# Prompt attention in a hybrid decoder step: items turned and weighed in batches of two, and narrow units scored into four single banks

## What is computed

```python
def attend_shared(q, k, v, dist, valid, rel_bias):
    logits = jnp.einsum('bqhgd,bkhd->bqhkg', qg, k).astype(jnp.float32) * ATTN_SCALE + bias
    p = masked_softmax(logits, valid[None, :, None, :, None])
    o = jnp.einsum('bqhkg,bkhd->bqhgd', p.astype(v.dtype), v)
...
def nsa_combine(gates, o_c, o_s, o_w):
    return gates[..., 0:1] * o_c + gates[..., 1:2] * o_s + gates[..., 2:3] * o_w
```

## Time and profile before

| | us |
|---|---|
| median of 3 runs (985.49 to 988.01) | 987.76 |
| span of the profiled execution, first to last instruction | 983.7 |
| median less that span (start and end of the program) | 4.06 |
| prompt attention within the span (its units and items) | 555.7 to 826.9 |

### The profile page before, as it was taken

One profiled execution on the slowest core, in us unless ns is written; L12 is line 12 of the kernel. 1 busy time (PEld: TensorE's weight loads), 2 busy tenths in 40 slices (PEclk: granted clock), 3 DMA queues, 4 the chain that ended last, 5 costly groups with the idle time before them and its releaser, 6 DMA issues. The chain is left out here.

```text
span 983.7 us, 15654 instructions
## 1 busy us (share of the span) xinstructions
PE 926.9 (94%) x5293; PEld 705.9 (72%) x5293; DVE 504.9 (51%) x1079; ACT 314.3 (32%) x699; POOL 191.3 (19%) x235
## 2 busy tenths in 40 slices
PE   7999989999999989999879998999999998999998
PEld 6676769998878777778579775666666665667784
DVE  4774253346344665450156357776666754564522
ACT  4222031223132334242110255555655553311100
POOL 1222222333102221110053102111011012343000
PEclk8999999999999999999979869999999999999999
DMA  7305811000621021312495410000000006788631
GB/s 263 132 17 117 213 42 46 2 1 1 233 115 49 22 65 47 106 43 94 114 207 154 104 47 22 22 22 22 1 22 1 22 18 219 225 224 294 207 103 48
DMA packets 90894, 91.13 MB, mean 93 GB/s; under 512 B 27630, under 2 KB 69534, under 8 KB 90454
## 3 DMA queue, kind: packets, MB, share of 16 engines
q1 hardware_dynamic: 70402, 71.60, 24.1%
q10 hardware_dynamic: 16700, 9.36, 3.5%
q0 software_dynamic: 3712, 9.17, 3.2%
HBM read 75.51 MB, written 23.49 MB: 101 GB/s over the span
## 5 line engine op out<-in xcount | busy, mean ns | idle before, releaser
L887 PE MATMUL ps<-w_high,x_high 128*128 128x512 f32 (+1 forms) x520 | 204.6, 393 | 2.3 <-DVE w_low L618 2.3
L889 PE MATMUL ps<-w_high,x_low 128*128 128x512 f32 (+1 forms) x520 | 199.8, 384 | 0.0
L888 PE MATMUL ps<-w_low,x_high 128*128 128x512 f32 (+1 forms) x520 | 199.3, 383 | 0.0
L887 PEld LDWEIGHTS ps<-w_high,x_high 128*128 128x128 f32 x520 | 98.1, 189 | 33.9 <-issue 12.9
L889 PEld LDWEIGHTS ps<-w_high,x_low 128*128 128x128 f32 x520 | 97.7, 188 | 20.9
L888 PEld LDWEIGHTS ps<-w_low,x_high 128*128 128x128 f32 x520 | 98.0, 188 | 18.9
L1718 PE MATMUL ps<-k_high,q_stack 128*128 128x512 f32 (+3 forms) x192 | 77.3, 406 | 12.1 <-DVE a_stats L1603 11.9
L399 POOL TENSOR_TENSOR stats<-stats,small 128x8 f32<-128x8 f32 (+3 forms) x35 | 41.7, 1190 | 213.9 <-DVE stats L670 159.3
L1718 PEld LDWEIGHTS ps<-k_high,q_stack 128*128 128x128 f32 x192 | 38.4, 200 | 53.2 <-DVE a_stats L1603 27.9
L1760 PE MATMUL ps<-weights_turned,v_nat 128*64 128x512 f32 x264 | 71.4, 622 | 0.0
L1719 PE MATMUL ps<-k_low,q_stack 128*128 128x512 f32 (+3 forms) x192 | 66.6, 354 | 0.0
(11 more groups left out here) (340 smaller groups left out, 1597.9 us busy)
## 6 DMA issues: line engine op xcount, KB each, us to landing
w_raw<-in_w_in SPq DMA_DIRECT2D x48, 256.0 KB, 4.4
tmp_skew<-tmp_table SPq DMA_DIRECT2D x8, 576.0 KB
bias_full<-tmp_skew SPq DMA_DIRECT2D x8, 512.0 KB, 5.0
w_out_raw<-in_w_out SPq DMA_DIRECT2D x16, 256.0 KB, 4.7
y_rows_in<-tmp_y SPq DMA_DIRECT2D x8, 512.0 KB, 4.5
x_rows<-in_x_prompt SPq DMA_DIRECT2D x8, 512.0 KB, 5.6
out_y_prompt<-out_rows SPq DMA_DIRECT2D x8, 512.0 KB, 5.4
x_tile<-in_x_prompt SPq DMA_DIRECT2D x6, 512.0 KB, 3.9
```

Of the source, the lines that this page charges most:

```text
L887: nc.tensor.matmul(out, s.xh[:, k, rows], s.wh[:, k, 0:w], start=(k == 0), stop=False)
L888: nc.tensor.matmul(out, s.xh[:, k, rows], s.wl[:, k, 0:w], start=False, stop=False)
L889: ins = nc.tensor.matmul(out, s.xl[:, k, rows], s.wh[:, k, 0:w], start=False, stop=(k == KT - 1))
```

## The change

Units of up to 512 keys, and the c units, take one bank of four, always the one used longest ago; wider units (640 keys and more, in tiles 4 to 7) take the pair 0-1 or 2-3 that was used longest ago. `score_after` holds the unit whose bias must be done.

Items are grouped into batches of at most two. Within a batch PE turns both items, then weighs the items of the batch before, then gives back a group whose last item was turned two batches before. DVE takes, per batch, the branch outputs of the groups that ended three batches before, then the copies, then the c outputs; ACT the copies, then `out_turned`. `due` is rounded to whole pairs, and the last unit of a group takes what is left. `weights_turned` gets a fourth buffer, and `edge_mask` moves to another place in memory for it.

```diff
-    RP, BANKS = 3, (4, 5, 7)
+    RP, BANKS = 4, (4, 5, 7)
...
-            due += [before + -(-fresh * max(0, j - 1) // (H - 2)) for j in range(H)]
+            first = 2 if t < WIN // P else 1
+            steps = [-(-fresh * max(0, j - first) // (H - 1 - first)) for j in range(H - 1)]
+            due += [before + c - c % 2 for c in steps] + [before + fresh]
...
+    batches = []
+    for i in range(n_u + 1):
+        k = due[i - 1] if i else 0
+        while k < due[i]:
+            batches.append((i, range(k, min(k + 2, due[i]))))
+            k += 2
...
+    for u, (_, br, _, n) in enumerate(units):
+        wide = br != "c" and P * n > 512
+        places = (0, 2) if wide else (0, 1, 2, 3)
+        used = lambda b: max(-1 if v is None else v for v in last_user[b:b + 1 + wide])
+        b = min(places, key=lambda b: (used(b), b))
+        score_bank.append(b)
+        score_after.append(used(b) + 1)
+        last_user[b:b + 1 + wide] = [u] * (1 + wide)
...
-                if u >= 2:
-                    pe.wait_ge(biased, u - 1)
+                if score_after[u]:
+                    pe.wait_ge(biased, score_after[u])
...
-                for k in range(done, upto):
-                    if k < n_k:
+                for n in at_step[i]:
+                    for k in batches[n][1]:
                         turn(k)
-                    if 0 <= k - LW < n_k:
-                        weigh(k - LW)
-                    gi = out_of(k - LB)
-                    if gi is not None:
+                    for k in earlier(n):
+                        weigh(k)
+                    for gi in ended_in(n - 2):
                         give_back(gi)
```

More of the change, by code:

```diff
@@ L1400, in attend_prompt @@
     one = m.put("ident_rounded", [P, P], F32R)
-    edge = m.put("edge_mask", [P, P])
+    edge = Memory(nc, SB_END + 4 * B * PAGES).put("edge_mask", [P, P])
     edge_r = m.put("edge_mask_rounded", [P, P], F32R)
@@ L1428, in attend_prompt @@
     c_item = [next(k for k, it in enumerate(items) if it == (2 * t, "c")) for t in range(TT)]
-    out_of = lambda k: items[k][0] if 0 <= k < n_k and items[k][1] != "c" and k + 1 == items_to[items[k][0]] else None
-    LW, LO, LB, LS = 2, 2, 4, 5
     HALF = T // 2
@@ L1433, in attend_prompt @@
     S_MIN, S_C, S_SUMS, S_SCALE, S_SUM = 0, 16, 48, 64, 80
-    tail = LS + 1
+    batches = []
[4 more added lines that the diff above has]
+            k += 2
+    n_b = len(batches)
+    batches += [(n_u, range(n_k, n_k))] * 3
+    batch_of = {k: n for n, (_, some) in enumerate(batches) for k in some}
+    at_step = [[n for n, (j, _) in enumerate(batches) if j == i] for i in range(n_u + 1)]
+    ended_in = lambda n: [gi for gi in range(n_g) if batch_of[items_to[gi] - 1] == n]
+    earlier = lambda n: batches[n - 1][1] if n else range(0)
+    score_bank, last_user = [], [None] * 4
+    score_after = []
+    for u, (_, br, _, n) in enumerate(units):
[6 more added lines that the diff above has]
+        last_user[b:b + 1 + wide] = [u] * (1 + wide)
     ring = []
-    for k in range(n_k + tail):
-        if k < n_k:
+    for n, (_, some) in enumerate(batches):
+        for k in some:
             ring += [((k, "c"), False)] if items[k][1] == "c" else [((k, 0), True), ((k, 1), False)]
[L1440 to L1443, removed]
+        ring += [((k, "sum"), False) for k in earlier(n) if items[k][1] == "c"]
+        ring += [((last, "out"), False) for last in [items_to[gi] - 1 for gi in ended_in(n - 2)]]
     turn_of = {key: r for r, (key, _) in enumerate(ring)}
@@ L1552, in _ @@
             nc.scalar.activation(edge_r[:], edge[:], ACT.Copy).then_inc(edge_kept, 1)
-            done = 0
             for i in range(n_u + 1):
@@ L1556, in _ @@
                     exp(i - 1)
-                upto = due[i] if i < n_u else n_k + tail
-                for k in range(done, upto):
-                    if k < n_k:
+                for n in at_step[i]:
+                    for k in batches[n][1]:
                         keep(k)
-                    gi = out_of(k - LO)
-                    if gi is not None:
+                    for gi in ended_in(n - 1):
                         keep_out(gi)
-                done = upto
         @block.vector
@@ L1577, in bias @@
                 dve.wait_ge(scored, u + 1)
-                pair = s.ps[:, 2 * (u % 2):2 * (u % 2) + 2, :].rearrange("p a c -> p (a c)")
+                pair = s.ps[:, score_bank[u]:score_bank[u] + (1 if P * n <= 512 else 2), :].rearrange("p a c -> p (a c)")
                 if br == "c":
@@ L1676, in _ @@
                     c_sums(i - 2)
[L1677 to L1680, removed]
+                for n in at_step[i]:
+                    for gi in ended_in(n - 3):
                         branch_out(gi)
-                    if k < n_k:
+                    for k in batches[n][1]:
                         keep(k)
-                    if 0 <= k - LW < n_k and items[k - LW][1] == "c":
-                        c_out(k - LW)
-                done = upto
+                    for k in earlier(n):
+                        if items[k][1] == "c":
+                            c_out(k)
             dve.wait_ge(y_ready, TT - 1)
@@ L1699, in score @@
                 t, br, h, n = units[u]
-                if u >= 2:
-                    pe.wait_ge(biased, u - 1)
+                if score_after[u]:
+                    pe.wait_ge(biased, score_after[u])
                 q = lambda h: s.qs[:, h, P * t:P * t + P]
-                b0 = 2 * (u % 2)
+                b0 = score_bank[u]
                 if br == "c":
@@ L1774, in _ @@
                 if i == 1:
[L1775 to L1778, removed]
+                    keep_clock(nc, s.ps[:, 3, :], s.qs[:, 0, 0:P], s.qs[:, 1, 0:512], 6)
+                for n in at_step[i]:
+                    for k in batches[n][1]:
                         turn(k)
-                    if 0 <= k - LW < n_k:
-                        weigh(k - LW)
-                    gi = out_of(k - LB)
-                    if gi is not None:
+                    for k in earlier(n):
+                        weigh(k)
+                    for gi in ended_in(n - 2):
                         give_back(gi)
-                done = upto
             keep_clock(nc, s.ps[:, 1, :], s.qs[:, 0, 0:P], s.qs[:, 1, 0:512], 12)
```

## The result

| | before | changed |
|---|---|---|
| median, us | 986.62 (983.75 to 988.01, 4 runs) | 1005.07 (1000.56 to 1007.57, 4 runs) |
| ratio to before, 95% interval | | 1.0191 [1.0161, 1.0221] |
| span of the profiled execution | 983.7 | 1004.8 |
| attention, first score to the closing matmuls (L1066) | 271.2 | 293.4 |
| of it tiles 0 and 1 / 2 and 3 / 4 to 7 with the end | 36.3 / 55.0 / 179.9 | 36.4 / 61.8 / 195.2 |

The stages in this and later tables are differences of starts of PE's rows in the timeline (first score of tiles 0, 2 and 4, first closing matmul).

The account below looks back on a forecast made before the run. PE's own list was taken as the bound. +12.5 us in tiles 4 to 7, +1.4 in tiles 0 to 3 and -0.4 at the end made +13.5; span 997.2 plus 4.06 around it gave 1001.3 us, range 984 to 1011.

Parts of the forecast that it names:

- Branch output: Tiles 4 to 7: six third sets of transposes wait for DVE's branch output, 9.8 us, less 0.46 lost already: 9.4.
- First f batches: Tiles 4 to 7, first batch of the four wide f groups: PE waits for ACT's copy, 5.9 us in all.
- Regular copies: Tiles 4 to 7: in ten pairs the fourth set of transposes waits for ACT's copy, 4.9 us in all.
- Joined weighings: Whole stage: 31 more weighings joined, 22 of them in tiles 4 to 7, save 0.15 each, 4.7 us.
- The joined turns: Whole stage: eight transposes behind eight others cost 0.88 us, not 0.99; 32 joins save 3.4 us.
- Scores in tiles 4 to 7: Shorter runs of scores without items at the start of a w group halve those four waits, saving 1.0 us.
- The end: End of the stage: joined work on PE saves 0.4 us.
- Tiles 0 to 3: Waits of 12.3 us, less 8.5 of earlier waits and 2.4 saved by joins: +1.4 us.
- the clock falls in the long waits: Rival: four long waits of tiles 2 and 3 each bring a slow-clock stretch of 1.6 us: 1007.7 us; chance 0.12.
- waits for ACT's copy: Sign of being right: PE's waits for ACT's copy appear before turns, some 10 to 12 us.
- waits for the branch output: Sign of being right: PE's waits for DVE's branch output appear before turns, some 10 to 16 us.
- The copies come in time: Rival: DVE and ACT catch up during PE's weighings, copy waits go, outputs cost 0.46: 976.6 us; chance 0.13.

Follow-up runs that it names:

- e8: e7 with PE, in the stage's last step, weighing the batch before ahead of turning the next: 980.03 us.
- e11: Changed kernel with PE's four long waits of tiles 2 and 3 filled with matmuls whose results nobody reads: 1002.08 us.
- e12: The changed kernel itself, unaltered, run again beside e11: 1006.96 us.
- e2: Changed kernel without the ring of four score banks, every unit scored into a pair of banks as before: 1008.57 us.
- e7: Changed kernel with ACT's copies ahead of the step's exponential and DVE's branch output at the start of the step behind the give-back: 982.53 us.
- e10: e8 with single items in tiles 0 to 3, and DVE's branch output behind the bias where the step behind a give-back holds no batch: 978.97 us.
- e5: Changed kernel with ACT's copies of a step ahead of the exponential of the unit before, DVE as it was: 995.98 us.

## Why the prediction was right, and where it was short

The direction, the mechanism and the place were right in tiles 4 to 7: PE, bound by its own list, waited in a ring of three. Of what was missing, most lies in tiles 2 and 3. The steps one by one, by the excess of each batch in the first profile:

- **Branch output, 9.8 us in six batches of tiles 4 to 7** (five at 1.56, one at 2.0): measured five at 1.58 to 1.60 and one at 2.05, 10.0 in all. The one row, carried over to the third set, priced them to 0.05 each.
- **First f batches, 5.9** (1.1, 1.35, 1.6, 1.8): measured 1.17, 1.43, 1.76 and 1.68, 6.0.
- **Regular copies, 4.9**: measured 4.4. Four of 0.45 (0.4 forecast), four of only 0.11 (first batches of the window groups, where PE had waited for a bias shortly before), and 1.05 and 1.08 for the two wide ones (0.65 and 1.05 forecast).
- **Joined weighings**, 23 of them at 0.15, 3.4 in tiles 4 to 7 and the end: PE's time in weighings fell from 53.1 to 49.3. The joined turns show only where no wait parts them, in e8.
- **Scores in tiles 4 to 7**: waits fell by 1.6 by the profile's gaps (1.0 forecast), but PE's whole time in scores, waits included, by only 1.2.
- **The end, -0.4: wrong.** The last group's first batch turns before it weighs, so PE waited 1.5 for the last unit's exponential, and 1.0 more for a branch output at its third set:

```profile
834.16 2.00 PE L1753 MATMUL ps<-ident,window_logits 128*128 128x128 f32 x16 [1.50 <-ACT window_logits L1554]
...
839.73 1.06 PE L1753 MATMUL ps<-ident,window_logits 128*128 128x128 f32 x8 [1.00 <-DVEq L1677]
```

In the kernel before, weighings stood there. I had counted only joins at the end; the two waits cost 2.9, nearly all of the step from the 12.1 forecast for tiles 4 to 7 and the end to the 15.3 measured. e8 took the first back: its wait there is 0.44.
- **Tiles 0 to 3, +1.4: undersized.** Measured +6.9, nearly all in tiles 2 and 3. The mechanism was the forecast one (the score waits moved into the batches), but the f batch of tile 2 waited 2.8 where 1.55 was set down, since DVE also had the compressed sums ahead of it, that of tile 3 waited 3.6 for 2.9, and the clock, for which I charged nothing, took some 4 us by the difference of e11 and e12.

So the rival "the clock falls in the long waits" came true beside the forecast, not in its place. For tiles 2 and 3 e11 and e12 show it, in one profile each. For tiles 4 to 7 two profiles of the same kernel differ: in the first, ten waits before turns, of 1.0 to 1.9 us, left the clock at 1.00; in e12 it was at half from 655.9 to 662.7 and from 754.9 to 758.3, and those tiles took 198.4 us instead of 195.2. A clock that falls there was one of the prediction's own signs of being wrong; that tiles 4 to 7 came out as near to the forecast as they did is in part the luck of the first profile. The Trainium skill (TensorE: Matmul & The Clock Gate, A second HAM failure mode: psum-queue depth-cycling) says that short idling of PE between groups of matmuls, while it cycles through PSUM banks, makes its clock swing between its two levels. The traces agree with it in tiles 2 and 3, and in tiles 4 to 7 in e12 but not in the first profile.

The row that I had weighed against this rival was misread besides: the eight waits of the earlier trace rows are not of 1.0 each but four of 0.95 to 1.12 and four of 0.31 to 0.58, and none could speak for waits three times as long. Of the other signs, waits for ACT's copy came to 9.2 us in all (10 to 12 forecast) and waits for the branch output to 20.0 (10 to 16 forecast), half of it in tiles 2 and 3. "The copies come in time" fell with the start of ACT's copies, as its own test said.

One slip in the base: I added 4.06 us around the span. Wherever a run's span and time are both listed, they differ by 1.6 to 1.7, so the profiled execution of before lay at some 985.4, below the median. Since 13.5 was in effect added to the median, the forecast is not touched, but the two profiled spans (21.1 apart) overstate the difference of the medians (18.5) by that and by the 1.4 by which the changed kernel's profiled execution lies above its own.

## What to carry to other kernels

Before joining steps on the bound engine, write down its buffer claims in their new order: the price of a batch is where the releasing operation stands in the other engine's list, not how long it takes, and it can be read from one place in the old trace where that release was late but covered. If the batch is worth having, reorder the releasing engines with it: here two edits of order on DVE and ACT gave back 18.8 us, as much as was lost. Time the parts of a change apart: one part was worth 7 us by itself and hidden behind the other. And read the granted clock of each stretch before a gain is put down to an edit: of those 7 us, 2.9 are shown at an equal clock.

## What the hardware showed

PE's clock fell to half in or behind some of its idle waits, and work without use in them held it up: in tiles 2 and 3 of e12 four waits of 1.7 to 3.6 us went with a granted clock of 0.92 over 61 us, and filled with 36 matmuls the same two tiles ran at 1.00 and 4 us shorter. But the length of a wait alone does not decide it. Windows at half clock in the kernel before (tile 3), e2 (tile 2) and e12 (tiles 4 and 6), columns again as in the earlier trace rows:

```profile
621.70:625.10 3.40, 3.40 (x12) 2.41 (x14) 3.02 (x11) 2.02 (x5) 0.00 (x0) 0.50 0.01 2
```

```profile
598.30:605.10 6.80, 5.71 (x23) 4.86 (x22) 4.34 (x15) 3.91 (x11) 1.79 (x2) 0.50 0.00 0
```

```profile
655.90:662.70 6.80, 6.08 (x25) 5.70 (x26) 4.64 (x13) 4.27 (x10) 0.00 (x0) 0.50 0.24 76
754.90:758.30 3.40, 3.40 (x10) 1.07 (x7) 0.32 (x1) 0.81 (x2) 0.00 (x0) 0.50 0.02 5
```

In the kernel before PE had waited 1.04 us just ahead; in e2 no wait in tiles 2 and 3 is longer than 1.3; the second of e12 follows a wait of 1.89, which left the clock at full in the first profile. In e7 to e10, with waits before turns of up to 1.6 in tiles 2 and 3, no half-clock stretch lies in those tiles. Not settled either is the start of tile 4: in e5 to e8, e11 and e12 the clock was at half for some 6.8 us there, in e2 for 3.4, in the other profiles it was not, though PE's scores wait 1.0 to 1.7 us there in all of them. No run was made on that.
